# A mixture-of-experts stage with six weight slots in place of four: experts as two transfers each, eight of them static, and blocks whose steps are no longer interleaved

## What is computed

```python
def hier_moe(h, w_rg, b_rg, w_re, b_re, w_gate, w_up, w_down):
    ...
    g_top = jnp.argmax(g_logits, -1)                 # one of 8 groups
    top_v, top_i = lax.top_k(e_logits, TOP_K_IN_GROUP)   # two of its 8 experts
    w = jax.nn.softmax(top_v, -1) * p_group
    ...
    def run_block(args):
        rows, e = args
        xb = x_pad[rows]
        hb = jax.nn.silu(xb @ w_gate[e]) * (xb @ w_up[e])
        return hb @ w_down[e]
```

## Time and profile before

| | |
|---|---|
| median of 3 runs | 1108.02 us (1105.99 to 1108.63) |
| profiled execution, its own time | 1108.65 us |
| its span in the profile | 1106.9 us |
| TensorE busy | 894.9 us (81%) |
| VectorE, ScalarE, GpSimd busy | 28%, 16%, 16% |
| mean granted TensorE clock | 0.932 of full speed |
| bytes moved by DMA | 253.28 MB, mean 229 GB/s |

### The profile page before, as it was taken

How to read it: one execution, slowest core, us unless ns; L and a number is a source line. 1 busy time by engine, 2 the same in 40 slices (tenths; PEclk the granted TensorE clock), 3 DMA queues, 4 the chain that set the end, 5 groups by cost and what they waited for, 6 DMA issues and landing times. The chain is left out here.

```text
span 1106.9 us, 14311 instructions
## 1 busy us (share of the span) xinstructions
PE 894.9 (81%) x4862; PEld 480.1 (43%) x4862; DVE 309.2 (28%) x769; ACT 182.0 (16%) x400; POOL 175.3 (16%) x271
## 2 busy tenths in 40 slices
PE   7999788989999999995398787877887878777610
PEld 3447674454444443454354444443444434444300
DVE  5960645740000011244411111110111011011145
ACT  1222156640000001002011111110110101011011
POOL 2000004420000000000122212221222212222103
PEclk9999988999999999997599999999999989999955
DMA  7332921039111110701049999999999999999231
GB/s 277 71 89 73 118 79 65 2 119 393 67 67 67 66 67 10 299 38 57 6 190 426 424 429 423 417 411 400 399 403 416 377 371 406 430 426 427 118 154 76
DMA packets 34372, 253.28 MB, mean 229 GB/s; under 512 B 14311, under 2 KB 14839, under 8 KB 24963
## 3 DMA queue, kind: packets, MB, share of 16 engines
q1 hardware_dynamic: 23668, 242.58, 55.4%
q0 software_dynamic: 10528, 9.72, 3.5%
q10 hardware_dynamic: 144, 0.55, 0.1%
HBM read 256.27 MB, written 21.04 MB: 251 GB/s over the span
## 5 line engine op out<-in xcount | busy, mean ns | idle before, releaser
L707 PE MATMUL ps<-arena,reg_a 128*64 128x256 f32 x1984 | 232.4, 388 | 69.8 <-DMA arena<-experts 67.9
L707 PEld LDWEIGHTS ps<-arena,reg_a 128*64 128x64 f32 x1984 | 148.7, 139 | 178.5 <-issue 121.6
L724 PE MATMUL ps<-arena,reg_a 128*64 128x512 f32 x496 | 126.1, 631 | 14.9 <-DVE reg_a L1426 14.9
L1426 DVE COPY reg_a<-ps 128x128 f32<-128x128 f32 x62 | 18.1, 291 | 389.3 <-PE ps L716 389.3
L605 PE MATMUL ps<-xT,arena 128*128 128x512 f32 x256 | 111.7, 594 | 2.1 <-PE ps L605 2.1
L1548 POOL DMA_INDIRECT ye_scratch<-reg_a,reg_u x62 | 62.2, 1003 | 219.7 <-ACT reg_a L937 210.5
L605 PEld LDWEIGHTS ps<-xT,arena 128*128 128x128 f32 x256 | 48.1, 190 | 65.6 <-issue 65.6
L937 ACT COPY reg_a<-ps 128x512 f32<-128x512 f32 x62 | 36.3, 585 | 186.4 <-PE ps L724 177.7
L931 ACT ACTIVATE reg_a<-ps 128x128 f32<-128x128 f32 x62 | 17.2, 277 | 289.2 <-PE ps L707 289.2
L724 PEld LDWEIGHTS ps<-arena,reg_a 128*64 128x64 f32 x496 | 31.2, 141 | 64.7 <-issue 43.6
L605 PE MATMUL ps<-reg_u,arena 128*128 128x512 f32 x128 | 57.5, 592 | 0.0
(11 more groups left out here) (241 smaller groups left out, 873.2 us busy)
## 6 DMA issues: line engine op xcount, KB each, us to landing
arena<-experts SPq DMA_DIRECT2D x62, 3072.0 KB
arena<-mid_w SPq DMA_DIRECT2D x8, 1792.0 KB, 7.4
reg_b<-front_w SPq DMA_DIRECT2D x12, 512.0 KB, 3.3
reg_a<-w_out SPq DMA_DIRECT2D x1, 4096.0 KB, 12.0
arena<-ye_scratch SPq DMA_DIRECT2D x4, 1024.0 KB, 8.9
xT<-x_t SPq DMA_DIRECT2D x8, 256.0 KB, 8.3
reg_b<-u_w SPq DMA_DIRECT2D x8, 256.0 KB, 9.1
arena<-shift_scratch SPq DMA_DIRECT2D x8, 256.0 KB, 11.0
```

The lines of the kernel that those rows point to most:

```text
L707: m = pe.matmul(ps[2 + k % 2][64 * h:64 * h + 64, 0:DE], xgT[k // 2][:, c, BLK * (k % 2):BLK * (k % 2 + 1)], slots[k][:, c * 512 + h * DE: ...
L724: m = pe.matmul(ps[6 + k % 2][64 * j:64 * j + 64, :], hT[k % 2][:, 64 * h:64 * h + 64], slots[k][:, KC * 512 + h * D + j * 512:KC * 512 + ...
```

## The change

- `NSLOT` goes from 4 to 6. The arena keeps its size; slot 4 lies in `reg_bo` (the old `reg_b` and `reg_o`, now one tensor) and slot 5 in `reg_a`. The small buffers of the stage move: `xg` to the end of `reg_a`, `xgT` and `yb` to `xT`, `gs`, `hb` and `hT` to the end of `reg_bo`, the gain and bias of the second norm from `xT` to `reg_u`.
- Each expert is two DMAs: gate and up (2048 KB, semaphore `s_wg`), then down (1024 KB, `s_wd`). The first waits for gate_up of the block that had the slot, the second for its down.
- `FORCED` goes from 4 to 8. Experts 4 and 5 are fetched into the new slots after the second write of `x1_dram`, once the output projection is done (`s_womm`); experts 6 and 7 after `s_idx`, the end of the routing, each as its slot comes free. With this input experts 4 to 7 all have tokens, so there are again 62 blocks, now 8 static and 54 extra.
- TensorE's step n is gate_up(n), turn_tokens for even n, turn_hidden(n), down(n). VectorE's is hidden(n), hidden_out(n), then tokens for even n. ScalarE and GpSimd follow block by block, and nothing is left over after the loop.
- The loop body holds `UN` = 12 steps, in 6 iterations: 72 conditions, of which 54 hold and the last 18 skip.

```diff
-FORCED = 4
+FORCED = 8
-NSLOT = 4
-EW = KC * 2 * DE + 2 * D
+NSLOT = 6
+UN = 12
+GU = KC * 2 * DE
+EW = GU + 2 * D
...
+        slots = [arena[:, EW * i:EW * (i + 1)] for i in range(4)] + [reg_bo[:, 0:EW], reg_a[:, 0:EW]]
+        ln2g, ln2b = reg_u[:, 0:D], reg_u[:, 1315:1315 + D]
...
+            def expert(e, k, need):
+                if need is not None:
+                    sp_.wait_ge(s_gu, need)
+                rows = slice(e * P, (e + 1) * P) if isinstance(e, int) else bass.ds(e, P)
+                sp_.dma_start(slots[k][:, 0:GU], a["experts"][rows, 0:GU]).then_inc(s_wg[k], 16)
+                if need is not None:
+                    sp_.wait_ge(s_dn, need)
+                sp_.dma_start(slots[k][:, GU:EW], a["experts"][rows, GU:EW]).then_inc(s_wd[k], 16)
...
             for t in range(TT):
                 sp_.wait_ge(s_ln1, t + 1)
                 sp_.dma_start(x1_dram[t * P:(t + 1) * P, :], x1t[:, t, :]).then_inc(s_x1d, 16)
+                if t == 1:
+                    sp_.wait_ge(s_womm, TT)
+                    for e in (4, 5):
+                        expert(e, e, None)
+            sp_.wait_ge(s_idx, 1)
...
+            for e in range(NSLOT, FORCED):
+                expert(e, e - NSLOT, e - NSLOT + 1)
...
-            with sp_.Fori(1, MAXB // 4) as i:
-                for k in range(4):
-                    with sp_.If(4 * i + (k - FORCED) < extra):
-                        e = sp_.value_load(ids[0:1, bass.ds(4 * i + k, 1)], min_val=0, max_val=(NE - 1) * P)
-                        sp_.wait_ge(s_dn, 4 * i + (k - 3))
-                        sp_.dma_start(slots[k], a["experts"][bass.ds(e, P), :]).then_inc(s_w[k], 16)
+            with sp_.Fori(0, (MAXB - FORCED) // UN) as i:
+                for j in range(UN):
+                    with sp_.If(UN * i + j < extra):
+                        n = UN * i + (FORCED + j)
+                        e = sp_.value_load(ids[0:1, bass.ds(n, 1)], min_val=0, max_val=(NE - 1) * P)
+                        expert(e, (FORCED + j) % NSLOT, n - (NSLOT - 1))
...
-            def step(i, k):
-                n = 4 * i + k
-                gate_up(i, k)
-                if not isinstance(n, int) or n >= 1:
-                    turn_hidden(n - 1, (k + 3) % 4)
-                if k % 2 == 0:
-                    turn_tokens(2 * i + (k // 2 + 1), (k // 2 + 1) % 2)
-                if not isinstance(n, int) or n >= 1:
-                    down(n - 1, (k + 3) % 4)
+            def step(i, c):
+                gate_up(i, c)
+                if c % 2 == 0:
+                    turn_tokens(6 * i + (c // 2 + 1), (c // 2 + 1) % 2)
+                turn_hidden(i, c)
+                down(i, c)
...
-            for k in range(4):
-                with pe.If(last == k):
-                    turn_hidden(extra + (FORCED - 1), k)
-                    down(extra + (FORCED - 1), k)
```

More of the change, by code:

```diff
@@ L215, in build_kernel @@
         lnst = ru.take(64)
-        re_ = Region(reg_a)
-        xg = [re_.take(D) for _ in range(2)]
-        xgT = [re_.take(KC * P).rearrange("p (c t) -> p c t", c=KC) for _ in range(2)]
+        xg = [reg_a[:, EW + D * i:EW + D * (i + 1)] for i in range(2)]
+        xgT = [xT[:, D * i:D * (i + 1)].rearrange("p (c t) -> p c t", c=KC) for i in range(2)]
+        yb = [xT[:, 2 * D + 512 * i:2 * D + 512 * (i + 1)] for i in range(4)]
+        re_ = Region(reg_bo, EW)
         gs = [re_.take(P) for _ in range(2)]
@@ L339, in _ @@
             for e in (0, 1):
-                sp_.dma_start(slots[e], a["experts"][e * P:(e + 1) * P, :]).then_inc(s_w[e], 16)
+                expert(e, e, None)
             for t in range(TT):
@@ L697, in turn_tokens, with gate_up, turn_hidden @@
                 m.then_inc(s_xt, 1)
-            def gate_up(i, k):
-                n = 4 * i + k
-                pe.wait_ge(s_w[k], 16 * i + 16)
-                pe.wait_ge(s_xe, 2 * i + (k // 2 + 1))
+            def gate_up(i, c):
+                n, k, q = UN * i + c, c % NSLOT, (c // 2) % 2
+                pe.wait_ge(s_wg[k], 16 * (2 * i + (c // NSLOT + 1)))
+                pe.wait_ge(s_xe, 6 * i + (c // 2 + 1))
                 if not isinstance(n, int) or n >= 2:
                     pe.wait_ge(s_h, n - 1)
-                for c in range(KC):
+                for x in range(KC):
                     for h in range(2):
-                        m = pe.matmul(ps[2 + k % 2][64 * h:64 * h + 64, 0:DE], xgT[k // 2][:, c, BLK * (k % 2):BLK * (k % 2 + 1)],
-                                      slots[k][:, c * 512 + h * DE:c * 512 + (h + 1) * DE],
-                                      start=(c == 0), stop=(c == KC - 1))
+                        m = pe.matmul(ps[2 + c % 2][64 * h:64 * h + 64, 0:DE], xgT[q][:, x, BLK * (c % 2):BLK * (c % 2 + 1)],
+                                      slots[k][:, x * 512 + h * DE:x * 512 + (h + 1) * DE],
+                                      start=(x == 0), stop=(x == KC - 1))
                 m.then_inc(s_gu, 1)
-            def turn_hidden(n, k):
+            def turn_hidden(i, c):
+                n = UN * i + c
                 pe.wait_ge(s_h, n + 1)
@@ L1564, in _ @@
             last = pool.value_load(ids[0:1, MAXB + 1:MAXB + 2], min_val=0, max_val=3)
-            with pool.Fori(1, MAXB // 4) as i:
-                for k in range(4):
-                    with pool.If(4 * i + (k - FORCED) < extra):
-                        step(i, k)
+            with pool.Fori(0, (MAXB - FORCED) // UN) as i:
+                for j in range(UN):
+                    with pool.If(UN * i + j < extra):
+                        step(i, FORCED + j)
             for k in range(4):
                 with pool.If(last == k):
-                    scatter(extra + (FORCED - 1), k)
                     n = extra + (FORCED - 1)
```

155 lines of the change are left out of this document (71 added, 84 removed).

## The result

The changed kernel takes **1079.68 us** (median of four runs, 1078.88 to 1082.25), against 1108.33 for the kernel before in the same rounds (1105.99 to 1111.06): a ratio of 0.974, 95% interval 0.970 to 0.977, so 2.6% less. The forecast was 1074 with a range of 1057 to 1092. The profiled execution has a span of 1077.4 us, 29.5 less than the 1106.9 of before, at a mean granted clock of 0.944.

The account below looks back on a forecast made before the run. Weight fetches were taken to bind the expert loop. Savings of 7.3 (start), 15.9 (two experts), 5.3 (no disturbance) and 10.3 (end), less 4.5 for shorter rows, gave 34.4 us less span and 1074 us, range 1057 to 1092.

Parts of the forecast that it names:

- What binds: In the expert loop: blocks wait for weights, with 1.7 us of TensorE slack each; two fewer experts there save 15.9 us.
- The start: Loop's first fetch: needs only gate_up of block 0, not its down, so it starts at 560.3 instead of 567.64, 7.3 us earlier.
- No disturbance: Loop's middle stretch: with five experts ahead of TensorE instead of three, late blocks no longer stop the fetches; 5.3 us saved.
- The surcharge for two transfers: Loop fetches: rows of 16 and 8 KB instead of 24 KB cost 0.08 us an expert, 4.5 us over 56.
- TensorE's own pace: Sequential steps in the loop: open chains add 0.91 and 0.73 us, giving 7.09 a block, under 8.04, so no cost.
- Body of twelve: Loop turns: going back to the top 4 times instead of some 15 changes the time by zero.
- The end: From the last weights to the read of the results: 12.7 us instead of 22.98, so 10.3 us saved.
- Gathers stay late: Rival, 11%: late gathers in the loop hold back all that follows on TensorE; 14 us more, 1088.
- The mean engine sets the pace: Rival, 10%: the mean DMA engine, not the slowest, paces the loop's fetches; 7.74 us a block, 1057.
- Every transfer has a price: Rival, 4%: each weight transfer costs up to 0.59 us, now paid twice; 28.6 us more, 1103.
- TensorE becomes the bound: Rival, 7%: open chains and a lowered clock make TensorE bind the loop, at 8.69 us a block, 1152.
- break-even: TensorE's pace in the loop at which no gain is left: 7.99 us a block, 0.90 over the forecast 7.09.

Follow-up runs that it names:

- a_late45: The changed kernel with experts 4 and 5 fetched behind the wait for gate_up of block 0 instead of during the router: 1095.93 us, ratio 0.987.
- a_rows_late: The changed kernel with the two loads of the second norm's rows issued behind experts 6 and 7, not at the end of the routing: 1082.91 us, ratio 0.975.
- b_split: The kernel before with each expert as two transfers with own semaphores, still four slots, four static experts and interleaved steps: 1107.36 us, ratio 0.997.
- a_single: The changed kernel with each expert as one transfer again, waiting for down of the block that had the slot: 1094.99 us, ratio 0.989.
- a_pe_plus: The changed kernel with two more matmul calls in each down, their results overwritten by the real ones: 1101.78 us, ratio 0.993.
- b_seq: The kernel before with a block's steps in sequence on all engines, still four slots, four static experts and single transfers: 1101.62 us, ratio 0.990.

## Why the prediction was right, and where its terms were off

- **What binds.** Right. Weights bind the second half of the stage (30 waits), and removing two experts from it gave 15.3 us where 15.9 stood (a_late45). The DMA shares that the prediction gives from 567.64 on are of rows that begin at 602.02.
- **The start, 7.3 predicted, 5.4 measured.** The mechanism held: the fetch starts as block 0's gate_up ends, at 562.24. But that gate_up began at 557.16 instead of 555.22. Of these 1.9 us, 0.8 are already in GpSimd's first copy (548.01 against 547.18), within what executions differ by there. The other 1.1 are the two loads of the norm's rows beside the first gather (a_rows_late), which the prediction didn't count.
- **"No disturbance", 5.3 predicted: the failed term.** The step was "a block that is a few microseconds late no longer stops the fetches", and so 7.96 an expert for the undisturbed stretches. The late gathers did vanish, but the pace did not follow: 8.11 against 8.10, and 8.15 in b_split, which has no gather wait either. By the sum made there (8.15 without a gain, 8.06 with all of it) b_split shows none of the 5.3 us and the kernel after at most 2. The prediction had read the stretches at 7.94 and 8.00 as the true pace and the one at 8.21 as damage. The mean over all of them was the pace of the last engines. Why the stretches of before differ is argued, not shown.
- **The surcharge for two transfers, 4.5 predicted.** Right in kind and about in size: 0.10 us of the engines' time for an expert, 5.6 us over 56 (a_single against after). Even so the split kernel is 0.17 us an expert faster than a_single, since the split also did the work that the prediction gave to the slots: it let the gathers through. The two terms together were to give +0.8; with the pace at 8.04 instead of 8.11 the fetch stretch was forecast 4.2 us too short, about 1 of it by the surcharge and the rest by the disturbance.
- **The Trainium skill** (SBUF — State Buffer, section on the DMA setup-cost knee) has about 2 us for each transfer, so an estimate from its figure is 2 us more for each expert. By that rule the trace does not agree: the second transfer costs 0.10 us, and the pace is 8.11 with two and 8.10 with one.
- **TensorE's own pace, 7.09 predicted.** Measured 6.98 over 30 blocks (565.56 to 774.93), with the open chain at 1.62 in an odd block (1020.15, the end of gate_up, to 1021.77), predicted 1.55. The first wait for weights came at block 32 (782.58), predicted 37. The chain costs nothing, but the cover was put too high: 0.95 us a block counts only once the lead is used up, and over the whole loop it is 0.55 (a_pe_plus).
- **Body of twelve.** Zero, as predicted, as far as the trace shows: from block 9 to block 31 gate_ups stand 7.00 or 7.01 apart, the loop's turns included.
- **The end, 10.3 predicted.** From the arrival of the last weights to the read it was to be 12.7 and was 1031.03 - 1018.70 = 12.3. Between gate_up of block 61 and the read 8.4 us were saved, and b_seq alone gives 8.1 of them.
- **The sum.** 5.4 + 15.3 + 8.4 + 0.4 = 29.5 against 34.4: 1.9 short at the start, 4.2 in the pace; the end gave 0.8 more than expected and the last row 0.4. The misses of 6.1 us outweigh the 1.2 that went the other way, so the time is in range because the large terms held (the start, the two experts, the end), not because errors cancelled.
- **The rivals.** "Gathers stay late" is what happens with one transfer (a_single: 1095), not here. "The mean engine sets the pace" failed as put, since the fast engines only run ahead and stop early; turning the rows around brings it about. "Every transfer has a price" of 0.59 us is excluded: it is 0.10. "TensorE becomes the bound" is the case in a_pe_plus: 0.88 us a block more bring 1101.8, on the way to the break-even that the prediction put 0.90 over its own 7.09.

**Open.** Which engines are last, and that they serve a block's first rows, was not read from a record of each engine; it is inferred from five kernels with other rows or fewer and from the DMA share at the end, which falls to that of two engines. What six slots give beyond room for two more experts was not tested.

## What to carry to other kernels

When a stage is bound by DMA, compare the mean bytes per engine with the pace: if fewer and fewer DMA engines are busy at its end while somebody still waits, the load is uneven, and the small transfers beside the large ones are the place to look. A wait that vanishes is worth nothing while another resource ends at the same time; ask of each stall what would have been waited for in its place. A load that is moved out of a short delay costs its full time if it lands in the stretch that transfers bind. Sequential steps make a shorter end and are free only while the engine that runs them stays under the mean time of a block, a lead at the start counted in; measure that margin by adding work until it shows.

## What the runs showed of the hardware

- GpSimd's gathers and scatters are 4.9% of DMA time, yet lift the pace of the weights beside them from at most 7.55 to 8.11 us; about 0.25 of that comes from which rows they use.
- Splitting the weight transfers decides here how long small ones beside them take: 30.9 us from a gather's issue to its landing with 3072 KB transfers in 24 KB rows, 10.1 us with 2048 and 1024 KB in 16 and 8 KB rows.
- The price of the split is small: 26.6 GB/s per engine with the single transfers (a_single), 26.3 with two (after).
- After waits of 2.00 to 2.47 us, four gate_ups of b_split took 5.34 to 5.36 us where 3.67 is usual, at a mean granted clock of 0.68 to 0.69. The wait alone doesn't decide: three others in the same run, after 2.10 to 2.31 us, took 3.67.
